# Rebuilding the expert stage of a diffusion-backbone layer: 15 row tiles, five weight buffers and an overflow round in the middle

## The reference, cut to what matters

```python
h = rms_norm(x, norm2_g) * (1 + sc2) + sh2
g_p, g_idx = top_k(softmax(h @ router_group_w + ...), 1)          # 1 of 4 groups
e_p, e_idx = top_k(softmax(logits of the group's 8 experts), 2)   # 2 of 8 experts
hid = silu(h @ w_gate[e]) * (h @ w_up[e])                         # 1024 -> 256, 32 experts
x = x + g2 * sum over the 2 picks of g_p * e_p * (hid @ w_down[e])
y = rms_norm(x, final_norm_g)
```

## Time and profile before

| what | value |
|---|---|
| median of 3 runs | 1041.59 us (1039.92 to 1042.72) |
| the profiled execution | 1038.34 us, its span 1036.6 us |
| PE, DVE, ACT, POOL busy in the span | 888.4, 589.8, 280.1, 64.5 us |
| mean granted TensorE clock | 0.878 |
| expert stage | from about 727 us to the end, some 310 us |
| loads of expert weights | 33 times 3 MB: 32 experts and one for the round |

### The profile page before, as it was taken

The page is one execution under the profiler, slowest core; times in us unless marked ns, Lnnn a source line. Parts: engine busy times, 40 slices in busy tenths (PEclk is TensorE's granted clock), DMA queues, the critical chain, the costliest instruction groups (busy, mean ns, idle before and its releaser), DMA issues.

```text
span 1036.6 us, 17411 instructions
## 1 busy us (share of the span) xinstructions
PE 888.4 (86%) x6868; PEld 542.5 (52%) x6868; DVE 589.8 (57%) x1183; ACT 280.1 (27%) x510; POOL 64.5 (6%) x74
## 2 busy tenths in 40 slices
PE   3999999799988896887898899997589797898787
PEld 2466555466666575666776664454433243343332
DVE  6259999865457766777665265756733233232326
ACT  4212010321655615566422244112000000000013
POOL 0100000000000000000000000000111111111013
PEclk9899999999988658676576699998699899999999
DMA  9962553232500300302004748411899999999875
GB/s 351 357 234 96 201 210 135 94 114 80 103 2 12 23 1 12 23 2 30 4 8 57 285 174 283 174 68 64 343 355 421 418 421 421 419 420 419 351 309 225
DMA packets 75871, 200.04 MB, mean 193 GB/s; under 512 B 42061, under 2 KB 44655, under 8 KB 61583
## 3 DMA queue, kind: packets, MB, share of 16 engines
q1 hardware_dynamic: 66416, 176.41, 47.1%
q0 software_dynamic: 7456, 17.09, 4.5%
q10 hardware_dynamic: 1919, 5.44, 1.3%
HBM read 183.88 MB, written 23.40 MB: 200 GB/s over the span
## 4 chain that ended last, share of the span: by engine, by line
PE 54%; DVE 22%; DMA 12%; ACT 7%; issue 3%; SPq 2%; DVEq 0%; ACTq 0%; POOLq 0%
PE bank L596 10%; DVE arena L1051 9%; PE bank L2422 9%; DMA arena<-in_expert_w_up 7%; PE bank L1687 6%; PE bank L2443 4%; PE bank L1308 2%; ACT arena L927 2%; PE bank L1365 2%; PE bank L1295 2%; DMA arena<-winv 1%; PE bank L1368 1%; PE bank L1320 1%; PE bank L1394 1%; DVE arena L1204 1%
## 5 line engine op out<-in xcount | busy, mean ns | idle before, releaser
L596 PE MATMUL bank<-arena 128*128 128x320 f32 x704 | 206.2, 446 | 2.4 <-ACT arena L417 2.4
L596 PEld LDWEIGHTS bank<-arena 128*128 128x128 f32 x704 | 132.8, 193 | 75.6 <-issue 25.3
L2422 PE MATMUL bank<-arena 128*64 128x512 f32 (+2 forms) x496 | 119.2, 628 | 16.6 <-DMA arena<-in_expert_w_up 15.6
L1051 DVE SCALAR_TENSOR_TENSOR arena<-arena 128x655 f32<-128x655 f32 x116 | 104.7, 902 | 4.5 <-DVE arena L1051 0.2
L2422 PEld LDWEIGHTS bank<-arena 128*64 128x64 f32 (+2 forms) x496 | 44.0, 145 | 89.9 <-issue 88.8
L2511 DVE TENSOR_TENSOR arena<-arena,bank 128x256 f32<-128x256 f32 x16 | 6.8, 422 | 116.8 <-ACT arena L2469 116.8
L1687 PE MATMUL bank<-arena 128*128 128x512 f32 x160 | 70.6, 595 | 0.0
L2443 PE MATMUL bank<-arena 128*64 128x512 f32 (+2 forms) x248 | 60.4, 613 | 9.4 <-DVE arena L2514 9.4
L2469 ACT ACTIVATE arena<-bank 128x256 f32<-128x256 f32 x16 | 6.2, 385 | 197.9 <-PE bank L2422 197.9
L2178 POOL DMA_INDIRECT arena<-tokens_for_experts,arena x17 | 17.4, 1022 | 492.0 <-DVE arena L2083 465.0
L1687 PEld LDWEIGHTS bank<-arena 128*128 128x128 f32 x160 | 29.6, 189 | 34.8 <-issue 34.6
(11 more groups left out here) (368 smaller groups left out, 1332.9 us busy)
## 6 DMA issues: line engine op xcount, KB each, us to landing
arena<-in_expert_w_gate SPq DMA_DIRECT2D x33, 1024.0 KB, 16.3
arena<-in_expert_w_up SPq DMA_DIRECT2D x33, 1024.0 KB, 19.1
arena<-in_expert_w_down SPq DMA_DIRECT2D x33, 1024.0 KB, 20.5
arena<-in_ada_w SPq DMA_DIRECT2D x12, 2048.0 KB, 10.5
arena<-in_w_in SPq DMA_DIRECT2D x22, 512.0 KB, 4.1
arena<-expert_rows SPq DMA_DIRECT2D x10, 512.0 KB, 8.2
arena<-in_w_out SPq DMA_DIRECT2D x1, 4096.0 KB, 15.7
arena<-modrows SPq DMA_DIRECT2D x8, 512.0 KB, 8.5
```

Source lines behind the costliest of these rows:

```text
L596: mm = nc.tensor.matmul(psum[4 + 2 * (n % 2) + half][:, 0:HALF], wring[:, n % NWIN, k], hT[:, k, half * HALF:(half + 1) * HALF], start=(pa ...
L1051: chain(nc.vector.scalar_tensor_tensor(acc, src, w, acc, ALU.mult, ALU.add))
L2422: mm = nc.tensor.matmul(psum[2 + n % 2][r, :], xeT[:, n % 2, c, r], gu[:, :, c, :], start=(c == 0), stop=(c == KD - 1))
```

## The change

- **Tiles.** 15 instead of 17. Rank 0 gets a third place of 32 rows (`TAIL`) in a tile with ranks 7 (64) and 8 (32), so it has room for 288; only rank 6 and the fixed experts also keep 64 rows; ranks 8 to 28 have 32 each, in five quads and that mixed tile. The order is now: fixed pair; fixed and rank 6; rank 1; quad; rank 0 twice; the mixed tile; rank 2; quad; rank 3; quad; rank 4; quad; rank 5; quad. A quad is last.
- **Overflow.** Its one round stands ahead of tile 9 (`OVAT`). With the counts above it holds no row. Its weights come by three indirect DMAs of POOL with one index per partition; for an empty round every index is out of bounds, so that no weight row is moved. POOL first fetches two tables, then issues four indirect DMAs; PE waits for all of them (`s_ovin`), as for the result of tile 8.
- **Loads.** Five buffers; the round takes turn 17 in their rotation, whose successor is turn 22. Turns whose buffers come free together form a group: all gates and ups first, then all downs. In numbers of turns the groups behind the first five turns are [5, 6] [7, 8] [9] [10 to 13] [14 to 16] [18] [19 to 21] [22] [23] [24 to 27] [28] [29 to 32]. Rank 0's third place keeps its buffer until tile 6 has used it.
- **Residual.** `x2` stays in SBUF: its five stores and its reload go. `fgain` is loaded before the weights, `gain_first` later than before.
- **End.** SP waits for tile 13's scatter, then reads the scattered rows while the last quad's weights land. PE passes the second pick's rows for three of the five token tiles, DVE adds them for the other two; six PSUM banks instead of four.
- **Router.** DVE gets four more operations on ranks and slots, and POOL's, PE's and ACT's programs follow.

```diff
+SINGLES = [(2 + m, ((1 + m, P),)) for m in range(NHOT - 1)]
+HOT = [(0, ((0, P),)), (1, ((0, P),)), (NHOT + 1, ((7, 64), (8, 32), (0, TAIL)))]
+PAIRED = [(NHOT + 2 + m, ((a, 64), (b, 64))) for m, (a, b) in enumerate(((FIXED, 6),))]
+QUADS = [(NHOT + 3 + m, tuple((9 + m + 5 * j, 32) for j in range(4))) for m in range(5)]
+NTILE = len(SINGLES) + len(HOT) + len(PAIRED) + len(QUADS) + 1
+NSLOT = NTILE + NOV
+ROWS = ([(NTILE - 1, ((FIXED + 1, 64), (FIXED + 2, 64))), PAIRED[0], SINGLES[0], QUADS[0]] + HOT
+        + [SINGLES[1], QUADS[1], SINGLES[2], QUADS[2], SINGLES[3], QUADS[3], SINGLES[4], QUADS[4]])
+OVAT = 9
...
-        NB = 6
+        NB = 5
...
+        def buffer_free(t, part):
 
             sp = nc.sync
...
+            if t < NB:
+                return
+            if LOADS[t - NB] == "overflow":
+                sp.wait_ge(s_gu, OVAT + 1)
+            elif part < 2:
+                sp.wait_ge(s_gu, LAST_USE[LOADS[t - NB]] + 1)
             else:
...
+                sp.wait_ge(s_edown, LAST_USE[LOADS[t - NB]] + 1)
+
+        def experts_load(turns):
+
+            sp = nc.sync
+            number = {}
+            for parts in ((0, 1), (2,)):
+                for t in turns:
+                    k, b = LOADS[t], ebuf[t % NB]
+                    buffer_free(t, parts[0])
...
+                    for m in parts:
+                        name = ("expert_w_gate", "expert_w_up", "expert_w_down")[m]
+                        sp.dma_start(view(b + 2048 * m, 2048), ins[name][0, bass.ds(number[t], 1)].rearrange(
+                            "o (p c) f -> p (o c f)", p=P)).then_inc((s_egu, s_edw)[m == 2][t % NB], 16)
...
+            chain(nc.vector.tensor_scalar(is_hot, room, float(P), None, ALU.is_gt))
+            chain(nc.vector.tensor_tensor(past, in_expert, room.unsqueeze(1).broadcast_to(B5), ALU.subtract))
+            chain(nc.vector.scalar_tensor_tensor(tail, past, float(-TAIL), is_hot.unsqueeze(1).broadcast_to(B5),
+                                                 ALU.is_ge, ALU.mult))
+            chain(nc.vector.scalar_tensor_tensor(less, tail, float(more), stride_less.unsqueeze(1).broadcast_to(B5),
+                                                 ALU.mult, ALU.add))
             dve.wait_ge(s_rows0, 1)
...
         def pool_overflow():
             pool = nc.gpsimd
             rounds = overflow_rounds(pool)
...
+            pool.wait_ge(s_slotst, 32)
+            pool.wait_ge(s_edown, LAST_USE[LOADS[OVTURN - NB]] + 1)
             with pool.Fori(0, rounds) as i:
...
+                pool.wait_ge(s_clear, i * 16 + 16)
+                pool.dma_start(rtab[:, 0:4].unsqueeze(1).bitcast(I32), slot_column(i + NTILE)).then_inc(s_rtab, 16)
+                pool.dma_start(rtab[:, 4:5].unsqueeze(1).bitcast(I32), weight_row(i), allow_slow_non_contiguous=True).then_inc(s_rtab, 16)
+                pool.wait_ge(s_rtab, i * 32 + 32)
                 pool.sem_inc(s_ovgo, 1)
...
+                pool.indirect_dma_start(out=eo[:, 2], out_offset=None, in_=h2d,
                                         in_offset=At(ap=rtab[:, 0:1].bitcast(U32), axis=0),
...
+                for m, name in enumerate(("expert_w_gate", "expert_w_up", "expert_w_down")):
+                    pool.indirect_dma_start(out=view(buffer + 2048 * m, 2048), out_offset=None,
+                                            in_=ins[name][0].rearrange("e (p c) f -> (e p) (c f)", p=P),
+                                            in_offset=At(ap=rtab[:, 4:5].bitcast(U32), axis=0),
+                                            bounds_check=last_weight, oob_is_err=False).then_inc(s_ovin, 16)
...
         def pe_overflow():
             pe = nc.tensor
             rounds = overflow_rounds(pe)
...
+            pe.wait_ge(s_eod, OVAT)
             with pe.Fori(0, rounds) as i:
...
+                pe.wait_ge(s_ovin, i * 64 + 64)
```

More of the change, by code:

```diff
@@ L1440, in build @@
         LOADS = []
-        for _tile, _ranks in ROWS:
-            LOADS += [k for k in _ranks if k not in LOADS]
-        LAST_USE = {k: n for n, (_tile, _ranks) in enumerate(ROWS) for k in _ranks}
+        for _n in range(NTILE):
+            if _n == OVAT:
+                LOADS.append("overflow")
+            LOADS += [k for k in ranks_of(_n) if k not in LOADS]
+        LAST_USE = {k: n for n in range(NTILE) for k in ranks_of(n)}
+        OVTURN = LOADS.index("overflow")
         tab = regp.take(NSLOT, 4)
@@ L1535, in gain_rows_load, with landings @@
             sp.dma_start(gain_step, modrows[1:2, 5 * D:6 * D].broadcast_to([P, D])).then_inc(s_fg, 16)
-        def turn_of(i):
-            return i if i < NEXP - len(ROWS[NTILE - 1][1]) else i + 1
-        def experts_load(i):
+        def landings(t):
+            return sum(LOADS[n] != "overflow" for n in range(t % NB, t + 1, NB))
+        def buffer_free(t, part):
             sp = nc.sync
[L1543 to L1546, removed]
-            else:
[L1548 to L1558, removed]
@@ new lines, in load_groups @@
+        def load_groups():
+            groups = []
+            for t in range(NB, len(LOADS)):
+                if t == OVTURN:
+                    groups.append([])
+                    continue
+                last = groups[-1][-1] if groups and groups[-1] else None
+                behind = (LAST_USE.get(LOADS[n - NB]) for n in (last, t)) if last else (0, 1)
+                first, second = behind
+                if last and (first == second or LAST_USE[LOADS[last]] == LAST_USE[LOADS[t]] == NTILE - 1):
+                    groups[-1].append(t)
+                else:
+                    groups.append([t])
+            return [g for g in groups if g]
@@ L1991, in build @@
[L1991 to L1996, removed]
+        OVP = (OVAT - 1) % 2
+        LAST_BUFFERS = [LOADS.index(k) % NB for k in ranks_of(NSTAT)]
+        spare = [b for b in range(NB) if b not in LAST_BUFFERS][0]
+        assert spare in [LOADS.index(k) % NB for k in ranks_of(NSTAT - 1)]
+        rege = Region(ebuf[spare], ebuf[spare] + EXPERT)
@@ L2508, in dve_experts @@
             turned(0)
-            for n in range(NSTAT):
+            for n in range(NTILE):
+                if n == OVAT:
+                    dve_overflow()
                 dve.wait_ge(s_silu2, n + 1)
@@ L2673, in _constants @@
     for tile, ranks in reversed(ROWS):
-        rows = P // len(ranks)
-        for j, k in enumerate(ranks):
-            first[1, k] = rows * sum(k in r for _, r in ROWS)
-            first[0, k] = P * tile + j + len(ranks) * first[1, k]
+        for k, w, _, stride, lane in slot_places(ranks):
+            if w < P and room_of(k) > P:
+                continue
+            first[1, k] = room_of(k)
+            first[0, k] = P * tile + lane + stride * first[1, k]
             first[2, k] = P * NTILE - first[0, k]
+    first[2, 0] -= tail_shift()[0]
     own = np.zeros(P)
```

381 lines of the change are left out of this document (156 added, 225 removed).

## The result

The changed kernel took 1049.2 us (median of 16 runs, 1042.74 to 1052.96), the kernel before 1041.59 in the same comparison. The ratio is 1.0081, 95% interval 1.0054 to 1.0108: slower by some 8 us, 2.9 us more than the 1046.3 predicted, and inside the range. The profiled execution took 1047.8 us with a span of 1046.1, against 1038.34 and 1036.6.

The account below looks back on a forecast made before the run. The prediction took weights and PE as nearly level bounds. Its five parts, tile 0 to the end, ran to 1041.3 against 1036.6, 4.7 us more; added to the median, 1046.3 us, range 1031 to 1056.5.

Parts of the forecast that it names:

- Part 1: Tiles 0 to 7: tile 0 starts as before at 749.1, tile 1's 1.69 us wait goes, tile 7's down ends at 852.4.
- Part 2: Tile 8: PE waits 2.6 us for weights, is done at 863.7 and frees turns 18 to 21, landed by 902.0.
- Part 3: Overflow round: PE stands 16 us for its inputs; tile 9's gate and up end at 912.4, queue empty since 902.
- the 3.3 of the row: POOL's indirect DMAs for the round: 3.3 us for each further one, from partly empty lists in the profile before.
- Part 4: From tile 9 to the last tile: 29 MB of weights take 3.9 + 83.2 us; the last down ends at 1015.1.
- Part 5: From the last down to the end: 26.2 us against 25.3 before; end at 1041.3, 4.7 us more.
- A: Rival at the overflow round, faster: empty transfers pass at once, weights alone bound the rest; 1032.0 us, chance 0.21.
- C: Rival at the overflow round, slower: each 8 KB weight row counts twice, 9.9 us more; 1056.2 us, chance 0.08.
- D: Rival at the overflow round: its weights are moved all the same, 3 MB and 8.6 us more; 1054.9 us, chance 0.05.
- B: Rival at the overflow round, no change: empties cost half of 3.3 us each, inputs 4.9 us sooner; 1041.4 us, chance 0.16.
- The bound of 0.3%: Whole-kernel time: a measurement can tell some 0.3%, 3.1 us, from no change.

Follow-up runs that it names:

- experiment 1: The changed kernel with the 64-row expert of the mixed tile (tile 6) computed as two matmuls of 32 columns; 1039.41 us, 1.0012 of the kernel before.
- Experiment 7: The changed kernel with tile 6's matmuls all 32 columns wide and POOL's part of the round one tile sooner; 1034.53 us (0.9932), again 1034.06 (0.9959).
- 10: Experiment 7's kernel with gate, up and down of each turn loaded before the next turn's gate; 1056.90 us, 1.0173 of the kernel before.
- experiment 6: The changed kernel with POOL's part of the round one tile sooner, tables read before the wait for the buffer; 1044.72 us, 1.0034 of the kernel before.

## Why the prediction was right, and where it was wrong

The sign and the size are right, by a sum in which one large term was missing and several were too large. That they cancel is luck. The kernel that the prediction priced, with every tile at 7.0 and 3.7 us, is that of experiment 1: its stage took 261.1 us where the sum had 266.0, and its time is not to be told from that before. So without the term that was missed, no slowdown would have been measured; the term added 6.3 us, and the stage became 267.4.

- **Part 1, "Tile 1 starts at 763.4, tile 6 at 827.0 and has done gate and up at 834.0".** This step failed. The tiles of one width follow at the pace forecast, but tile 3 waited 3.40 us for its weights and then ran 1.7 us at the lower clock, where the forecast had it just in time; and tile 6 was priced like the others, 7.0 and 3.7 us, without a word, though no row of before shows a tile of two widths. Nothing bounded it. Measured 15.95 and 8.01. Gate and up ended at 849.5, 15.5 us late, of which 8.9 are the two widths and 5.1 tile 3. The gather's 1.69 us wait went and the queue ran empty near 756, as forecast.
- **Part 2, tile 8 done at 863.7.** 879.6, later by the same amount, and bound by PE rather than by weights.
- **Part 3.** The tables were put at 9.9 us; 4.2, because the mixed tile had emptied the queue. Without that hole they took 8.2 (experiment 1), and 11.6 in 7 (846.51 to 858.08): the forecast lies among the values of a full queue. The four indirect DMAs: 19.1 forecast, 15.4 measured, the first 7.7 and the others 2.6 each. The wait: 16 forecast, 11.48 measured. The round with its low clock: 18.8 forecast, 16.9 measured (896.91 to 913.78). POOL had begun the tables 19.8 us late (877.38, forecast 857.6), since tile 7's result was; these three terms took back 11.3 of that. By the Trainium skill (DMA: Bandwidth & Descriptors, Queues, rings and completion order) the prediction estimated some 2.5 us for each empty transfer; 2.6 was measured for each further one, so the estimate by the Trainium skill was nearer than the 3.3 of the row; whether its mechanism is the cause, no run here shows. Tile 9's gate and up ended at 920.8 instead of 912.4, with the hole behind them.
- **Part 4.** 29 MB from there took 83.1 us where 87.1 were put: 4.0 back. The waits ahead of tiles 10, 12 and 14 were forecast as about 4, 8 and 10 us, and are 3.14, 7.12 and 10.77. The last down ended at 1019.0, forecast 1015.1.
- **Part 5.** 26.2 forecast, 27.1 measured. DVE's timeline of the change:

```profile
1019.96 0.75 DVE L2482 SCALAR_TENSOR_TENSOR arena<-bank,arena 128x512 f32<-128x512 f32 x1
1022.89 0.69 DVE L2573 TENSOR_TENSOR arena<-arena,bank 128x512 f32<-128x512 f32 x1 [2.18 <-PE bank L2547]
...
1026.33 0.69 DVE L2573 TENSOR_TENSOR arena<-arena,bank 128x512 f32<-128x512 f32 x1 [2.02 <-PE bank L2547]
...
1027.78 2.56 DVE L2583 SCALAR_TENSOR_TENSOR arena<-arena 128x1024 f32<-128x1024 f32 x1
...
1033.14 1.23 DVE L2571 TENSOR_TENSOR arena<-arena 128x1024 f32<-128x1024 f32 x1
```

and POOL's last addition:

```profile
1026.88 2.37 POOL L2306 TENSOR_TENSOR arena<-arena 128x1024 f32<-128x1024 f32 x1 [0.15 <-DMA arena<-expert_rows]
```

The first sum comes 3.9 us after the down and the two additions take 1.23 each, as put. Not foreseen: one of DVE's scalings takes 2.56 us instead of 1.28 while POOL adds beside it, and DVE is not without a pause.

**The rivals.** A's mechanism fell: empty transfers do not pass at once, 7.7 us for the first. Its condition, tile 9 done before the queue runs dry, was to decide between faster and slower. Alone it does not: experiment 6 all but meets it and stays at 1.0034, since the mixed tile has cost its part. Experiment 7 meets it with the mixed tile mended and gets 1034 us, where A had 1032.0. C and D fell: the further transfers cost 2.6 us, less than 3.3, and POOL's queue moved not a megabyte more. As a price B was nearest: 14.2 us for the four (19.1 less 4.9), 15.4 measured (15.0 to 16.1 in four other traces). So the end at +4.7 in the forecast became +9.5 between the two profiled executions: 2.4 from the front, 5.2 in the stage, 1.8 at the end. The bound of 0.3% that I gave for a measurement fits the comparison of the change (0.27% to either side) and is too fine for the experiments: single runs of one kernel spread over 10 to 20 us, and with fewer runs the intervals reach 0.56% to either side.

## What to carry to other kernels

Before a tile of two column widths is packed, price it as one tile for each width; if the weights are there anyway, cut the wide one down to the narrow one. With few buffers look for every place where the release of buffers stands behind something slow (a round's inputs, an odd tile): such holes in the transfers hide one another, so that mending one shows only a part of its worth. And a stage measured inside the trace tells changes of a few us that the whole time, with a front that moves by 9 us, does not; here 2 us were at its edge.

## What the runs showed of the hardware that I had not expected

- Matmuls of 64 and of 32 columns never ran side by side on TensorE: at each change of width the next start came 0.52 us after the last one. Two widths in one tile took 14.07 us grouped by width and 15.95 in turn, one width 7.08; each change of width some 0.13 us, in gate and up and in down alike.
- An indirect DMA of POOL whose indices are all out of bounds moves no row and still took 7.7 us from issue to PE's start under load (one trace), 2.6 for each further one behind it. POOL's queue carried 17.09 MB with the three loads of weights and without them, but 7344 packets against 6912: 144 for each.
- Two small table loads on POOL's queue took 4.2 us beside a queue half empty (154 GB/s in 876 to 882), and 8.2 to 12.5 us beside full ones (experiments 1 and 10).
- A scaling of DVE over 128 x 1024 took 2.56 us (2.26 in 7) while POOL added in SBUF, 1.28 otherwise. DVE's sums out of PSUM took 0.69 us beside POOL's additions and without them (1022.89 and 1034.40).
